# One attention stage in place of three: prompt tiles of both mixers and paged-cache chunks, one of each per step

## The reference, cut to what matters

```python
s = q @ k.T * 64**-0.5 - slope * dist          # masked above the diagonal, 1024 x 1024 per map
p = softmax(s)                                 # A: w = p[0] - lam * p[1]; o = w @ v (128 wide)
                                               # B: o = p @ v (64 wide), two heads to a unit
```

```python
kp = cache_k[page_table]      # 8 x 4096 keys x 4 heads x 128, 256 KB for one page
vp = cache_v[page_table]      # the same size
w = diff_weights(concat(scores(q, kp), scores(q, k_new)), lam);  o = w @ concat(vp, v_new)
```

## Time and profile before

| | us |
|---|---|
| median of 3 runs (lowest, highest) | 3925.64 (3924.53, 3928.91) |
| the profiled execution, its own time | 3928.74 |
| its span | 3927.2 |
| PE busy in the span | 3241.9 (83%) |
| DVE busy | 2798.5 (71%) |
| ACT busy | 1213.3 (31%) |
| POOL busy | 1220.6 (31%) |
| moved by DMA | 992.67 MB, mean 253 GB/s |

### The profile page before, as it was taken

One profiled execution on the slowest core, in us unless ns is written; L12 is line 12 of the kernel. 1 busy time (PEld: TensorE's weight loads), 2 busy tenths in 40 slices (PEclk: granted clock), 3 DMA queues, 4 the chain that ended last, 5 costly groups with the idle time before them and its releaser, 6 DMA issues. The chain is left out here.

```text
span 3927.2 us, 63929 instructions
## 1 busy us (share of the span) xinstructions
PE 3241.9 (83%) x22587; PEld 2878.6 (73%) x22587; DVE 2798.5 (71%) x6620; ACT 1213.3 (31%) x2349; POOL 1220.6 (31%) x1219
## 2 busy tenths in 40 slices
PE   7997769666646777764755999999999999999998
PEld 5776547523323555553655999999999999999998
DVE  6562644211102488889854999999999999999998
ACT  5442435312202232225972222222222222222221
POOL 0000000024432000000003556565756555555554
PEclk9998989877867888887987999999999999999999
DMA  4323122299978432323999999999999999999997
GB/s 140 113 73 95 56 64 66 101 357 387 387 263 312 145 108 96 125 70 101 330 303 335 340 331 345 346 343 332 351 352 334 335 345 356 336 335 344 347 334 281
DMA packets 405587, 992.67 MB, mean 253 GB/s; under 512 B 38002, under 2 KB 165972, under 8 KB 404116
## 3 DMA queue, kind: packets, MB, share of 16 engines
q0 software_dynamic: 150048, 595.57, 41.6%
q1 hardware_dynamic: 253140, 385.63, 28.2%
q10 hardware_dynamic: 2224, 9.44, 0.6%
HBM read 911.56 MB, written 146.44 MB: 269 GB/s over the span
## 5 line engine op out<-in xcount | busy, mean ns | idle before, releaser
L1852 PE MATMUL banks<-x_hi,u_hi 128*128 128x320 f32 x2048 | 634.1, 310 | 62.6 <-DVE x_lo L1942 62.6
L1865 PE MATMUL banks<-coef_hi,v_hi 128*128 128x320 f32 x2048 | 633.8, 309 | 6.1 <-issue 6.1
L1852 PE MATMUL banks<-x_hi,u_lo 128*128 128x320 f32 x2048 | 633.8, 309 | 0.0
L1852 PE MATMUL banks<-x_lo,u_hi 128*128 128x320 f32 x2048 | 633.8, 309 | 0.0
L1865 PE MATMUL banks<-coef_lo,v_hi 128*128 128x320 f32 x2048 | 633.6, 309 | 0.0
L1865 PE MATMUL banks<-coef_hi,v_lo 128*128 128x320 f32 x2048 | 633.6, 309 | 0.0
L1813 POOL DMA_INDIRECT uv_row<-in_v_rows,expert_tok x384 | 478.8, 1247 | 382.5 <-DVE y_tok L1996 328.0
L1813 POOL DMA_INDIRECT uv_row<-in_u_rows,expert_tok x384 | 462.1, 1203 | 358.5 <-DVE dots L1970 308.4
L1996 DVE SCALAR_TENSOR_TENSOR y_tok<-uv_row,share,y_tok 128x1024 f32<-128x1024 f32 x415 | 530.3, 1278 | 0.7
L1970 DVE CUSTOM_DVE_ANT_0 uv_row<-uv_row,x_tok 128x1024 f32<-128x1024 f32 x416 | 506.4, 1219 | 0.0
L1852 PEld LDWEIGHTS banks<-x_hi,u_hi 128*128 128x128 f32 x2048 | 385.4, 188 | 62.8 <-DVE x_lo L1942 62.8
(11 more groups left out here) (267 smaller groups left out, 5519.5 us busy)
## 6 DMA issues: line engine op xcount, KB each, us to landing
keys_sa<-in_cache_k SPq DMA_DIRECT2D x256, 256.0 KB
values_sa<-in_cache_v POOLq DMA_DIRECT2D x256, 256.0 KB, 6.7
uv_raw<-in_u SPq DMA_DIRECT2D x128, 512.0 KB
uv_raw<-in_v SPq DMA_DIRECT2D x128, 512.0 KB
scratch_gates<-stage SPq DMA_DIRECT2D x10, 4096.0 KB, 29.9
gates<-scratch_gates SPq DMA_DIRECT2D x128, 320.0 KB
out_win_k_out<-in_state_k POOLq DMA_DIRECT2D x8, 4088.0 KB
out_win_v_out<-in_state_v POOLq DMA_DIRECT2D x8, 4088.0 KB
```

What stands on the lines that cost most here:

```text
L1852: ins = nc.tensor.matmul(bank[:, 2 * r + c, 0:CH], u[r][a][:, k * P:(k + 1) * P], x2[b][:, k, c * CH:(c + 1) * CH], start=(k == 0 and a == b),
L1865: ins = nc.tensor.matmul(bank[:, 4 + n % 4, 0:CH], v[j][a][:, k * P:(k + 1) * P], coef[j][b][:, c * CH:(c + 1) * CH], start=(j == 0 and a ...
```

## The change

The three phases prompt A, prompt B and sample A become one, `attend_both`. It runs 74 steps. Step n has on every engine a share of prompt tile n (64 tiles: the 32 of A, then the 32 of B) and a share of the cache chunks: chunk n is scored, chunk n - 8 is transposed and chunk n - 9 meets its values. The last 10 steps have no tile. What changes in detail:

- The row tiles of a unit come in the order 7, 0, 6, 1, 5, 2, 4, 3 instead of 0 to 7.
- Both score maps of a tile share one pair of banks (0 and 1) instead of having a pair each. The second map's matmuls stand behind the first one or two groups of transposes and wait until DVE has read the first map. Transposes use banks 2 and 3, cache transposes bank 4, cache scores bank 5, cache values bank 6, and prompt outputs bank 7, one bank instead of two.
- The values of tile n are now multiplied in step n, not n + 1. Biased scores, exponentials and (for A) weights share one buffer, in place.
- All `q_blocks` of the samples are made once at the start; the copy of them for each batch (L972) is gone. Scores, exponentials and transposed exponentials of the cache are held in place in `past_exps` and in two small buffers `past_exps_T`.
- SP issues in one order: key pages of chunk m, in some steps the five loads of the next unit, then the store of prompt tile m - 5. POOL issues the value pages. ACT issues the load of the cache bias (2 MB) at the start.
- The loops are written out (no register loops), so every wait is on a constant.

In the diff, `is_a(n)` is true for the first 32 tiles, `maps(n)` is 1 for A and 2 for B, and `groups(n)` is 1 for tiles of up to four blocks and 2 for larger ones. Functions of the cache (`past_scores`, `transpose_past`, `past_values`, `fold`, `bias_past`, `past_exps`, `take_past_T`) hold the instructions of the old sample stage; `combine(n)`, `exps(n, m)` and `take_weights_T(n, x)` those of the prompt stage.

```diff
+def attend_both(nc, io, sems, ident, bank, neg_lam):
...
+        QT = SEQ // P
+        ORDER = (7, 0, 6, 1, 5, 2, 4, 3)
+        N = 2 * UNITS * QT
+        A_TILES = UNITS * QT
+        CHUNKS = DB * C_A
+        KEYS = PAST
+        R = 4
...
+        wT = sb("weights_T", [P, 2, QT, P])
...
+        es = sb("past_exps", [P, KEYS + DQ])
+        eT = sb("past_exps_T", [P, 2, 4, P])
...
+            sp.dma_start(pages[:, :], io["page_table"]).then_inc(pages_loaded, 16)
+            sp.wait_ge(zeroed, 4)
+            load_unit(0)
+            sp.dma_start(qs[:, :, :], io["qkT"][0:4, :, SEQ:NT].rearrange("h p t -> p h t")).then_inc(consts_loaded, 16)
...
+            for m in range(CHUNKS):
+                load_k(m)
+                if m == R:
+                    load_unit(1)
+                if m % QT == R + 1 and m > QT:
+                    sp.wait_ge(o_in_psum, m // QT * QT)
+                    load_unit(m // QT + 1) if m // QT + 1 < 2 * UNITS else None
+                if m > R:
+                    store(m - R - 1)
...
+            def scores(n, m):
+                buf, i = n // QT % 2, row_tile(n)
+                if n % QT == 0 and m == 0:
+                    pe.wait_ge(loaded[buf], 80 * (n // QT // 2 + 1))
+                since(pe, s_biased, 2 * n + m)
+                for c in range(0, (i + 1) * P, 512):
+                    width = min(512, (i + 1) * P - c)
+                    ins = nc.tensor.matmul(bank[:, c // 512, 0:width], q[buf][:, m, i * P:(i + 1) * P],
+                                           k[buf][:, c:c + width], start=True, stop=True)
+                ins.then_inc(s_in_psum, 1)
...
+            def transpose_group(n, x):
+                i, g = row_tile(n), group_before[n] + x
+                m, j0 = x // groups(n), 4 * (x % groups(n))
+                if is_a(n):
+                    pe.wait_ge(w_ready, n + 1)
+                else:
+                    pe.wait_ge(exp_done, 2 * n + m + 1)
+                since(pe, wT_ready, g - 1)
...
+            def weigh_values(n):
+                buf, i = n // QT % 2, row_tile(n)
+                since(pe, o_ready, n)
...
+            def past_scores(m):
+                t = m // C_A
+                pe.wait_ge(k_loaded[m % R], 64 * (m // R + 1))
+                pe.wait_ge(setup, 11)
+                since(pe, biased, m)
...
+            for n in range(CHUNKS + 10):
+                t, s = n // C_A, n % C_A
+                tile = n < N
+                every = maps(n) * groups(n) if tile else 0
+                if n + 1 < N:
+                    scores(n + 1, 0)
+                for x in range(min(2, every)):
+                    transpose_group(n, x)
+                if n + 1 < N:
+                    scores(n + 1, 1)
+                for x in range(2, every):
+                    transpose_group(n, x)
+                if 0 <= n - 9 < CHUNKS:
+                    past_values(n - 9)
+                if s == 1 and t > 1:
+                    fold(t - 2)
+                if s == 1 and 1 <= t <= DB:
+                    transpose_new(t - 1)
+                if s == 3 and t < DB:
+                    new_scores(t)
+                if tile:
+                    weigh_values(n)
+                if 0 <= n - C_A < CHUNKS:
+                    transpose_past(n - C_A)
+                if n < CHUNKS:
+                    past_scores(n)
...
+            def bias_scores(n, m):
+                buf, L = n // QT % 2, (row_tile(n) + 1) * P
+                dve.wait_ge(s_in_psum, 2 * n + m + 1)
+                if n % QT == 0:
+                    dve.wait_ge(loaded[buf], 80 * (n // QT // 2 + 1))
+                since(dve, wT_in_psum, group_before[n - 1] if n else 0)
+                nc.vector.memset(gate[:, 2 * n + m:2 * n + m + 1], 0.0)
+                nc.vector.tensor_tensor_reduce(
+                    e[:, n % 2, m, 0:L], bank[:, 0:2, :].rearrange("p b c -> p (b c)")[:, 0:L],
+                    strip[buf][:, m % maps(n), SEQ - L:SEQ], -1.0, 3e38, ALU.add, ALU.min,
+                    neg_max[:, n % 2, m:m + 1]).then_inc(s_biased, 1)
...
+            def output(n):
                 par = n % 2
-                dve.wait_ge(o_in_psum, turn * TURN_TILES + (n + 1))
-                since(dve, o_stored[par], turn * (8 * TURN_TILES) + 16 * (n // 2))
-                if a:
-                    nc.vector.tensor_copy(o[:, par, :], bank[:, 6 + par, 0:P]).then_inc(o_ready, 1)
+                dve.wait_ge(o_in_psum, n + 1)
+                since(dve, o_stored[par], 16 * (n // 2))
...
+            for n in range(CHUNKS + 10):
+                t, s = n // C_A, n % C_A
+                if n + 1 < N:
+                    bias_scores(n + 1, 0)
+                    bias_scores(n + 1, 1)
+                if s == 1 and 1 <= t <= DB:
+                    scale_of(t - 1)
+                if s == 1 and t > 1:
+                    take_folded(t - 2)
+                if s == 3 and t < DB:
+                    bias_new(t)
+                if s == 4 and t + 1 < DB:
+                    new_keys(t + 1)
+                if n + 1 < N:
+                    combine(n + 1)
+                if s == 0 and t > 1:
+                    scale_rows(t - 2)
+                if n < N:
+                    output(n)
+                if n < CHUNKS:
+                    bias_past(n)
+                    if s == C_A - 1:
+                        take_max(t)
...
+            for n in range(CHUNKS + 10):
+                t, s = n // C_A, n % C_A
+                tile = n < N
+                every = maps(n) * groups(n) if tile else 0
+                if n + 1 < N:
+                    exps(n + 1, 0)
+                for x in range(min(2, every)):
+                    take_weights_T(n, x)
+                if n + 1 < N:
+                    exps(n + 1, 1)
+                for x in range(2, every):
+                    take_weights_T(n, x)
+                if s == 1 and 1 <= t <= DB:
+                    take_new_T(t - 1)
+                if s == 0 and 1 <= t <= DB:
+                    past_exps(t - 1)
+                if 0 <= n - C_A < CHUNKS:
+                    take_past_T(n - C_A)
...
-        phase(attend_prompt, ident, bank, neg_lam, "a")
-        phase(attend_prompt, ident, bank, neg_lam, "b")
-        phase(attend_sample, ident, bank, neg_lam, "a")
+        phase(attend_both, ident, bank, neg_lam)
```

More of the change, by code:

```diff
@@ L409 @@
 UNITS = 4
-QT = SEQ // P
-NB = 2
 def lambda_column(nc, io, sems, out):
@@ L552, in _ @@
+            pool.wait_ge(pages_loaded, 16)
+            for j in range(CHUNKS):
+                load_v(j)
+                if j % C_A == R:
+                    load_v_new(j // C_A)
+                if j % C_A == R + 1 and j > C_A:
+                    store(j // C_A - 1)
+            store(DB - 1)
+            pool.wait_ge(past_o_stored, 16 * DB)
         @block.tensor
         def _(pe):
[L554 to L563, removed]
@@ L608, in _ @@
-            turns(pe, TURNS, turn_of)
+            def past_scores(m):
[3 more added lines that the diff above has]
+                since(pe, biased, m)
+                since(pe, new_biased, (m - 3) // C_A + 1)
+                since(pe, past_o_ready, (m - 17) // C_A + 1)
+                for h in range(4):
+                    ins = nc.tensor.matmul(bank[h * PR:(h + 1) * PR, 5, :], q_all[:, t, h, :],
+                                           kbuf[m % R][:, :, h, :], start=True, stop=True)
+                ins.then_inc(scored, 1)
@@ new lines, in fold @@
+            def fold(t):
+                pe.wait_ge(rows_scaled, t + 1)
+                pe.wait_ge(biased, min(C_A * t + 17, CHUNKS))
+                since(pe, new_biased, min((C_A * t + 17 - 4) // C_A + 1, DB))
+                since(pe, past_o_ready, t)
+                for h in range(4):
+                    ins = nc.tensor.matmul(bank[0:DQ, 5, h * P:(h + 1) * P], sel[:, h, :], o_rows[:, 0:P], start=True, stop=True)
+                ins.then_inc(folded, 1)
+            scores(0, 0)
+            scores(0, 1)
@@ L671, in _, with bias_past @@
-            turns(dve, TURNS, turn_of)
+            def bias_past(m):
+                c = m % C_A
+                dve.wait_ge(scored, m + 1)
+                since(dve, e_transposed, m - C_A + 1)
+                at = slice(c * 4 * P, (c + 1) * 4 * P)
+                nc.vector.memset(gate[:, 2 * N + m:2 * N + m + 1], 0.0)
+                nc.vector.tensor_tensor_reduce(es[:, at], bank[:, 5, :], bias[:, at], -1.0, 3e38, ALU.add, ALU.min,
+                                               mins[:, c:c + 1]).then_inc(biased, 1)
```

421 lines of the change are left out of this document (260 added, 161 removed).

## The result

The changed kernel takes 3872.7 us (median of four runs, 3861.5 to 3876.2), the kernel before 3926.4 (four runs, 3924.5 to 3928.9). The ratio is 0.9857, with an interval of 0.9845 to 0.987. It is 53.7 us faster. I had forecast 3800: the direction and the wide range held, but the gain is under half of the 126 forecast, and outside the forecast's own range (3765 to 3840). 3873 is also, to the microsecond, the time of the rival of the middle clock. The experiments show that this is chance: with two more output buffers and nothing else changed, 112 us of it go.

The account below looks back on a forecast made before the run. Three stages with different limits (DMA, PE, a DVE/ACT chain) left engines idle; merged, PE bounds. Start 29, A 271, B 291, reloads 25, end 32, barrier 8.5 make 656.5 against 781 us: about 3800, range 3765 to 3840 (8 in 10: 3705 to 3880).

Parts of the forecast that it names:

- the rival of the middle clock: In the merged steps, interruptions keep PE's mean clock grant at 0.85 in both halves: 3873 us, chance 0.20.
- the rival that nothing overlaps: PE instructions waiting for pages or a store hold up both kinds of work: 3900 to 3925 us, chance 0.04.
- The step model: The 64 steps with a tile: 8.3 us each in A and 9.1 in B, stalls included.
- SP's order: At each unit reload the store lands behind five more DMAs, DVE 4 us late: six times, 25 us, bounds 0 to 50.
- That is hidden, by little: In an ordinary step the store lands about 6 to 7 us in, and DVE wants it at 8.
- The clock: PE's grant in the merged steps: 0.95 in A, costing 10 us, and 1.00 in B.
- my own sign for "wrong": The forecast is wrong if, among other signs, the stage's window shows a clock grant under 0.9.
- The stalls between PE and DVE: PE's waits on DVE in the merged steps: 3.1 us per pair of steps in A, 1.4 in B.
- my second and third stall: In A's tile pairs, PE waits 1.4 us for merged weights, then about 1.0 for DVE, late out of that merge.
- The rival in which PE never waits: In the merged steps the engines drift until every result is ready in time: gain 246 us, 3680, chance 0.18.
- The start: Before the merged steps, loads sharing the DMA engines, query preparation and tile 7's chain take 29 us (16 to 40).

Follow-up runs that it names:

- the best version: Four output buffers, the store ahead of a unit's loads and the first value pages asked for later, against the changed kernel: 3743.9 us, ratio 0.9541.

## Why the prediction was wrong in its size

**What bounds, and the overlap: right.** The DMA engines fill while PE works, pages are never late in the middle, and the rival that nothing overlaps (3900 to 3925) fell. The step model held once the waits for stores were out of the way. From tile 7 to tile 7 (start of its first bias on DVE, in us):

| unit | A1 | A2 | A3 | A4 | B1 | B2 | B3 |
|---|---|---|---|---|---|---|---|
| forecast | 53 (66 less 13) | 66 | 66 | 66 | 73 | 73 | 73 |
| changed | 64.5 | 84.6 | 82.9 | 85.3 | 86.2 | 84.5 | 85.1 |
| four buffers | 60.4 | 66.3 | 63.5 | 66.1 | 69.6 | 70.4 | 70.4 |

The forecast's units already hold eight steps each without the reload stall. Without the waits for stores A2 to A4 came out as forecast and B 3 us shorter per unit; A1 was 7 longer. The 18 us that I added to A for ScalarE's exponentials and the clock didn't show: by halves the steps took 252 and 284 us there, against 271 and 291.

**The step that failed: "SP's order", 25 us of stalls with a bound of 50.** The place, once per unit reload, was right; six times 4 us was the mis-sized term. All waits for stores together are worth 112 us by four buffers and 118 by stores from ScalarE. The units with a reload are 14 to 19 us longer than with four buffers (102 us of the 108 in the steps), and A1 and the last B, without one, 4 and 2 us. The term was also added up wrongly. Its own parts, 3.7 us of issue, 3.3 more, about 7 of transfer and 1.6 of landing, make 15.6 and not 12.5, unless the transfer runs beside the issue, which the prediction doesn't say. By 15.6 DVE would have been 7.6 us late, 46 us in all. The measured 18.2 is beyond that too. At the stall shown above, counted from the issue of the key pages at 494.50:

- The store's issue began at 5.5 us; I had 7.0. The issue of loads was priced well.
- The issue was held for 6.6 us; I had nothing. Rows 8 only show an issue under a steady stream of pages, and rows 9 only how late the landing was (8.2), not what held it. The trace of the kernel before had a sign of it: the tenth load of two units in a row took 3.4 us to issue.

```profile
570.14 3.40 SPq L523 DMA_DIRECT2D strip_b<-in_strips  x1
```

- From there it landed in 6.2 us; I had 5.5. It was there at 18.2, not at 12.5.
- DVE wanted it at 3.3; I had 8. I had counted 8 us, a whole step, from the scoring of the chunk that releases the key pages. That chunk's scores ended at 492.9, SP's first page came 1.6 us later, and the output is wanted before the cache transposes and scores that close the step. So it was 14.9 us late, not 4.

**"That is hidden, by little": wrong.** An ordinary step also waited, in 32 places, since a landing takes 5.1 us in this stage and 1.6 was taken from one where the DMA engines stood at 25%. Alone that costs little: A1 waits 6.0 us for stores and loses 4.1, the last B waits 14.7 and loses 2. In the reload units both kinds count: the waits are 181 us there, and 102 us are lost. Moving the store one chunk earlier removes all the ordinary ones and over half of the long ones' sum, for 70 us.

**The clock: the observation right, the cause not.** The grant was 0.85 in A's half of the steps and 0.94 in B's, below the 0.95 and 1.00 that I took, and over the stage's window it was 0.87, so my own sign for "wrong" (under 0.9) came. But by that rival the clock is low because every step is interrupted. With four buffers A's steps still are: from 463 to 659 PE waits 29 times for DVE, up to 2.8 us long, and the grant over it is 0.97, where the changed kernel had 0.86. From 650 to 930 it is 1.00, with 35 waits of at most 1.0 us, where the changed kernel had 0.91. So the clock followed the waits for stores. Which of them, isn't separated: over the same 280 us it was 0.95 with only the six long ones left (the store one chunk earlier, up to 9.3 us) and 0.91 with the store ahead of the loads, 41 waits of up to 11.4 us. What it cost: for the same matmuls PE was busy 522.2 us in the stage and 500.1 with four buffers, so 22 of the 108 us are PE's own work at a lower clock (the rival had 83 against a full clock), and the rest is idle time. The Trainium skill's rule on gaps from cycling through banks (TensorE: Matmul & The Clock Gate, "A second HAM failure mode: psum-queue depth-cycling") would have kept the clock swinging all through, where the banks are still cycled with short gaps. In B's half, at 1.00, these runs don't bear it out; in A's the clock did fall for short spells (0.80 from 463 to 480 us), but at 0.97 over 196 us they cost little.

**The stalls between PE and DVE: somewhat too large.** Without the reload term the sum was 631.5 us for the stage, and with four buffers it is 617.6: 26 less in the steps (536 after 562), 7 more at the start, 5 more at the end and the barrier. The chain of the merge, my second and third stall, was worth 7 to 9 us in all and not the 2.4 per pair of A's 16. The rival in which PE never waits (3680) fell: the best version, with nothing late at SP, has 3744.

**The start: 36 and not 29 us.** I had counted the loads that share the DMA engines, and not that POOL's 16 value pages get in front of the unit that PE needs. Holding them back gave 15.5 us. A small slip in the same sum: 5.3, 2.7 and 0.3 make 8.3 us for a step of B and not 8.4, which is 3 us over its 32 steps.

**Left open.** The hold and the landing behind it are parts of one wait; no run changed the size of the unit's loads, so it isn't shown how much of the 18 us is the volume of those loads, how much their number, and how much the value pages that POOL moves beside them. Nor is it settled why the kernel with the earlier store ahead of the loads loses only 22 us of stage to four buffers, in the profiled executions, with 33 us more of waits for stores and 8 more of PE's busy time, where the kernel with the earlier store alone and the one with three buffers lost about the sum.

## What to carry to other kernels

When transfers that were in separate stages come onto one queue, price a small store by the landing and the issue under the merged traffic, behind the largest burst of loads, and ask how many steps later its buffer is wanted: here two more buffers of 64 KB, or one other issuing engine, were worth twice what the merge itself brought. A number that matches a rival proves nothing until a run takes that rival's cause away or leaves it in. Among the waits of an engine, count the long ones apart from the many short ones. Here the short ones alone cost little (A1 and the last B: 20.7 us of waits, 6 lost), and where only the long ones were left, they cost about their length and some clock in two kernels, and less in a third.

## What the runs showed of the hardware that was not expected

- A DMA's issue is not a fixed cost. On SP it took 0.33 to 0.43 us as a rule, and 5.1 to 10.3 us (changed kernel and four buffers) directly behind four 256 KB pages and the 2.1 to 2.6 MB of a unit. Behind the first unit's 2.1 MB alone it took 5.65 us with 4 MB of value pages asked for at the same time, and 0.92 without. The time goes to whatever comes next on that engine: the store, or with the store moved ahead, a key page (6.9 us).
- A 64 KB store lands in 5.1 us at the median at a DMA share of 0.7 to 0.8, from SP or from ScalarE alike, and in 1.6 with the DMA engines at a quarter.
- The granted clock rose from 0.91 to 1.00 over the same 280 us once stalls of 14 to 19 us, one per 85 us, and the waits of up to 6.3 us between them were gone, with 35 waits of up to 1.0 us left. With 29 waits of up to 2.8 us in 196 us it was 0.97.
